# Building narrow one-hots as eight per-token instructions, and dropping a wait between dot products, in a PEER decoder layer

## The reference

```
q = (h @ w_query)                          # 8 heads, two halves of 128
s_top, i_top = top_k(q . sub_keys, 16)     # per head and half, of 128 keys
best, pos = top_k(s_top[0] + s_top[1], 16) # of the 16 x 16 pairs
expert = i_top[0] * 128 + i_top[1]         # 16384 experts
gate = softmax(best)
act = gelu(u[expert] . x)                  # u: 16384 x 2048
out = sum over 8 heads x 16 of gate * act * v[expert]   # v: 16384 x 2048
```

## Time and profile before

| what | value |
|---|---|
| median of 3 runs | 2019.93 us (2019.1 to 2022.46) |
| the profiled execution, its own time | 2017.72 us |
| its span in the trace | 2015.8 us |
| VectorE busy | 1363.1 us, 68% of the span |
| GpSimd busy | 1045.7 us, 52% |
| TensorE matmul busy | 1780.5 us, 88% |
| transfers | 647.28 MB |

### The profile page before, as it was taken

The page is one execution under the profiler, slowest core; times in us unless marked ns, Lnnn a source line. Parts: engine busy times, 40 slices in busy tenths (PEclk is TensorE's granted clock), DMA queues, the critical chain, the costliest instruction groups (busy, mean ns, idle before and its releaser), DMA issues.

```text
span 2015.8 us, 18828 instructions
## 1 busy us (share of the span) xinstructions
PE 1780.5 (88%) x6299; PEld 1127.8 (56%) x6299; DVE 1363.1 (68%) x2189; ACT 574.0 (28%) x1039; POOL 1045.7 (52%) x643
## 2 busy tenths in 40 slices
PE   7999999999999999875655588898887899999997
PEld 6888888888888898622222233444343554444442
DVE  5464453223334338898998888788888888887956
ACT  5445453345543520210000032233313730000001
POOL 4443343444432413575555555565556768876733
PEclk9999999999999999887777898999998999999999
DMA  8986455665545689999999999999999999999997
GB/s 211 242 176 145 146 188 149 196 195 181 169 154 184 196 278 407 376 412 420 414 420 417 402 404 396 409 403 412 400 413 416 393 381 406 405 410 380 402 422 313
DMA packets 157641, 647.28 MB, mean 321 GB/s; under 512 B 25894, under 2 KB 31086, under 8 KB 95598
## 3 DMA queue, kind: packets, MB, share of 16 engines
q0 software_dynamic: 73728, 450.98, 55.1%
q1 hardware_dynamic: 83824, 195.16, 31.1%
HBM read 729.91 MB, written 2.10 MB: 363 GB/s over the span
## 4 chain that ended last, share of the span: by engine, by line
PE 46%; DMA 25%; DVE 16%; issue 7%; POOL 6%; ACT 1%; SPq 0%; DVEq 0%; POOLq 0%; ACTq 0%
PE acc L1539 10%; PE acc L1541 10%; PE acc L1540 10%; DMA v_low<-in_peer_v_dram,idx 7%; DMA v_high<-in_peer_v_dram,idx 5%; DMA u_ring<-in_peer_u_dram,idx 5%; PE misc L1888 4%; PE acc L1868 3%; DVE y_sum L1420 3%; DMA v_more<-in_peer_v_dram,idx 2%; DVE u_ring L1386 2%; DVE u_ring L1388 2%; DMA u_mid<-in_peer_u_dram,idx 2%; PE acc L1829 1%; DMA late_hot<-in_peer_v_dram,idx 1%
## 5 line engine op out<-in xcount | busy, mean ns | idle before, releaser
L530 POOL TENSOR_TENSOR w_lo<-raw,w_hi 128x1024 fp32r<-128x1024 f32 x112 | 274.3, 2450 | 424.7 <-ACT w_hi L640 424.4
L1888 PE MATMUL misc<-v_high,diag 128*128 128x512 f32 x512 | 272.7, 683 | 99.7 <-DMA v_high<-in_peer_v_dram,idx 94.0
L1539 PE MATMUL acc<-w_hi,t_hi 128*128 128x512 f32 x896 | 354.9, 396 | 0.0
L1541 PE MATMUL acc<-w_hi,t_lo 128*128 128x512 f32 x896 | 349.3, 390 | 0.0
L1540 PE MATMUL acc<-w_lo,t_hi 128*128 128x512 f32 x896 | 348.7, 389 | 0.0
L1888 PE MATMUL misc<-v_low,diag 128*128 128x512 f32 x512 | 269.8, 679 | 85.8 <-DMA v_low<-in_peer_v_dram,idx 76.2
L988 DVE TENSOR_TENSOR w_lo<-raw,w_hi 128x1024 fp32r<-128x1024 f32 x112 | 154.2, 1377 | 265.0 <-ACT w_hi L640 264.9
L640 ACT ACTIVATE w_hi<-raw 128x1024 fp32r<-128x1024 f32 x224 | 236.9, 1059 | 329.9 <-PE acc L1541 283.8
L572 POOL DMA_INDIRECT u_ring<-in_peer_u_dram,idx x160 | 204.3, 1277 | 183.8 <-DVE dots L1388 121.3
L1888 PEld LDWEIGHTS misc<-v_high,diag 128*128 128x128 f32 x512 | 107.1, 219 | 250.9 <-DMA v_high<-in_peer_v_dram,idx 127.2
L1386 DVE CUSTOM_DVE_ANT_0 u_ring<-u_ring,hn 128x1024 f32<-128x1024 f32 x160 | 195.8, 1223 | 68.4 <-DMA u_ring<-in_peer_u_dram,idx 60.4
(11 more groups left out here) (273 smaller groups left out, 2170.3 us busy)
## 6 DMA issues: line engine op xcount, KB each, us to landing
u_ring<-in_peer_v_dram SPq DMA_DIRECT2D x48, 1024.0 KB, 8.9
raw<-in_w_in_dram SPq DMA_DIRECT2D x64, 512.0 KB, 6.7
raw<-in_xattn_wk_dram SPq DMA_DIRECT2D x32, 512.0 KB, 4.4
raw<-in_xattn_wv_dram SPq DMA_DIRECT2D x32, 512.0 KB, 3.9
raw<-in_w_out_dram SPq DMA_DIRECT2D x32, 512.0 KB, 4.7
raw<-in_xattn_wq_dram SPq DMA_DIRECT2D x32, 512.0 KB, 4.7
raw<-in_xattn_wo_dram SPq DMA_DIRECT2D x32, 512.0 KB, 4.8
praw<-in_peer_wq_dram SPq DMA_DIRECT2D x24, 512.0 KB, 7.2
```

The lines of the kernel that those rows point to most:

```text
L530: nc.gpsimd.tensor_tensor(w_lo[:, j % RING, :, :], raw[:, j % RING, :, :], w_hi[:, j % RING, :, :].bitcast(F32), ALU.subtract).then_inc(lo ...
L1539: nc.tensor.matmul(o, xh, w_hi[:, s, kk, :], start=first, stop=False)
L1541: ins = nc.tensor.matmul(o, xl, w_hi[:, s, kk, :], start=False, stop=last)
L1888: ins = nc.tensor.matmul(o, diag[:, n % 4, :], v_slot(n % VS)[:, i * CW:(i + 1) * CW], start=False, stop=False)
```

## The change

In a batch, VectorE made `hotB` with two instructions over [rows, 8, 48]: compare the token's first key (broadcast over 48) with the keys (broadcast over 8 tokens), wait for that, and multiply by the weight (broadcast over 48), in place. Now there are eight instructions, one for each token, over [rows, 48]: each reads one tensor operand, the keys, compares it with a scalar per partition, the token's first key, and multiplies by a second scalar per partition, its weight. There is no wait between them, and the last raises `hot_ready`. The wait for `dot_done` in the last three groups is gone.

```diff
-                step(nc.vector.tensor_tensor(hotB[0:rows, q, :, :], listsT[0:rows, 0, t:t + WB].unsqueeze(2).to_broadcast([rows, WB, DENSE]),
-                                             keys[0:rows, FROM:].unsqueeze(1).to_broadcast([rows, WB, DENSE]), ALU.is_equal))
-                nc.vector.tensor_tensor(hotB[0:rows, q, :, :], hotB[0:rows, q, :, :],
-                                        listsT[0:rows, 2, t:t + WB].unsqueeze(2).to_broadcast([rows, WB, DENSE]),
-                                        ALU.mult).then_inc(hot_ready, 1)
+                for i in range(t, t + WB):
+                    ins = nc.vector.tensor_scalar(hotB[0:rows, q, i - t, :], keys[0:rows, FROM:], listsT[0:rows, 0, i:i + 1], listsT[0:rows, 2, i:i + 1],
+                                                  ALU.is_equal, ALU.mult)
+                ins.then_inc(hot_ready, 1)
...
                     dve.wait_ge(u_landed[u_index(n)], 16 * u_turn(n))
-                    if g >= GROUPS - WHOLE - 1:
-
-                        dve.wait_ge(dot_done, n)
```

## The result

The changed kernel takes 2032.4 us as the median of 6 runs (2030.56 to 2034.19), the kernel before 2019.9 us (2017.12 to 2022.46): a ratio of 1.006, 95% interval 1.005 to 1.0071, 12.5 us slower by the medians. The forecast was 2020.4 us, no change, with a range to 2027. The profiled execution took 2034.19 us, its span is 2032.3 us.

What follows compares the result with a forecast made beforehand. Transfers on the 16 DMA engines were taken as the bound. At 1607 us, 4.0 - 0.35 - 4.1 = -0.4 us, nothing late; +0.5 taken from 0 to +2.4 gave 2020.4 us after 2019.93, range 2015.5 to 2027.

Steps and rivals of the forecast that it cites:

- What bounds the kernel: From near 800 us the expert part waits for transfers; groups 14 and 15 lose only 2.2 us of full transfer.
- The prediction's own sign of being wrong: A DMA share under 0.95 in groups 14 and 15 would show the forecast wrong; 0.97 and more, right.
- The removed wait: Between neighbouring dots of groups 13 to 15: 0.05 us each, 1.0 us in all, 0.35 before 1607 us; can't lose.
- the sum: VectorE's lateness at 1607 us: 4.0 - 0.35 - 4.1 = -0.4 us, +1.8 at the top; overall 0 to +2.4.
- The cost of a batch: Eight narrow instructions at 0.18 us take 1.44 us against 1.06 before: +0.4 us a batch.
- Where it falls: Block 0's sixteen batches, 6.4 us more, cost nothing under waits for `u`; block 1's first ten add 4.0 us.
- the 4.1 us of slack: VectorE's waits in block 1 before 1607 us: 2.3 for GELU, 0.5 for TensorE, about 1.3 for `u`.
- Rival B: Slower: VectorE and GpSimd hold each other up at batches in groups 14 and 15; +4.6 us, 2025 us; chance 0.09.
- A: Slower: the eight instructions do not overlap, 0.3 us each, +1.3 us a batch; +10 us, 2030 us; chance 0.07.
- C: Faster: the scalars cost nothing, a batch takes 0.65 us, -0.41; about 2017.7 us; chance 0.17.
- D: Only the order of gathers shifts, moving others a few us either way; beyond 2 us to either side, chance 0.09.

Runs made afterwards that it cites:

- e1: Kernel before with only the wait for dot_done removed, old pair of one-hot instructions kept; 2025.73 us, ratio 1.003.
- e12: Changed kernel with one wait added after each eight narrow instructions of block 1; 2024.12 us, ratio 1.0024.
- e7: Changed kernel with one scalar per partition instead of two, weight left out, so it does not compute the layer; 2026.81 us, ratio 1.0035.
- e2: Kernel before with only the eight narrow instructions put in, wait for dot_done kept; 2023.4 us, ratio 1.0016.
- e6: Kernel before, all waits kept, with three extra narrow instructions into an unused place ahead of each pair; 2022.62 us, ratio 1.0014.
- e5: Kernel before with the eight narrow instructions, wait for dot_done kept, and one more wait after the fourth of the eight; 2027.3 us, ratio 1.0034.
- e9: Kernel before without the wait between dots, with one wait after each pair of block 1 instead; 2019.99 us, ratio 1.0.
- e8: Kernel before without the wait between dots, dot halves in groups 14 and 15 plain one-tensor sums, not computing the layer; 2018.67 us, ratio 0.9992.

## Why the prediction was wrong

- **What bounds the kernel: right.** Transfers do, and most of the loss went where VectorE has no cover, into groups 14 and 15: 12.1 us more of lost transfer time. The prediction's own sign of being wrong, a DMA share under 0.95 there, came with 0.86 and 0.88.
- **The removed wait: the step that failed.** "So it is worth 0.05 us", and "It can't lose". Both are wrong. The size came from a gap of 0.18 us in group 12, taken for the state without the wait. The changed kernel still shows 0.20 us at that place, so something else made it, most likely the wait for the row of `u`; between neighbouring dots of group 14 its gap is 0.00, so the wait had been worth 0.23 us at each pair of dots. And it can lose, because GpSimd needed that gap: the term stood in the sum as 0.35 us won, and the runs show about 6 us lost (e1; 7.6 us between the changed kernel and e12). The argument for "can't" looked at VectorE's own slots alone, and not at the engine that issues the gathers.
- **The cost of a batch: right in kind, at the top of its range.** Forecast 0.18 us an instruction, between 0.145 and 0.21; measured 0.21. The second scalar costs nearly what the first does (e7). A batch is 1.71 - 1.06 = 0.65 us longer, not 0.4. (The lower value should read 0.14: 0.08 us for 128 columns makes 0.05 for 80. It changes nothing here.)
- **Where it falls: block 0's batches are free**, as forecast. The DMA share from 1190 to 1530 us is 1.00 in both kernels; VectorE is busy 9.3 us longer there (282.02 against 272.74) and waits 6.9 us less for `u` (47.9 against 54.8 over all its slots). Group 14 starts with its lists copied at 1536.93 against 1534.84 us, the 2.1 us that the first group had already. In block 1 the 4.1 us of slack hid less than counted: in e2 the last dot is summed at 1642.8 us, 3.3 us later than before, and the added work costs about 3 us (e2, e6), where the sum had 0 to 2.4.
- **Rival B named the right pair of engines and the wrong instructions.** It had VectorE's narrow instructions wait for GpSimd, or the reverse, for up to 1.4 us a batch. In fact GpSimd waits for the dots behind a batch, and these were there all along. A sign of it stood in the trace before, issues of 0.95 us beside others of up to 3.35 us; the prediction did not ask what made them long. It gave B 0.09 and 2025 us.
- **Rivals A and C: ruled out.** The eight do overlap (0.21 us from start to start, a median of 304 ns each), and the scalars are not free. A's time, 2030 us, is near the measured one, but not by A's cause: e2 and e6, which have the added work alone, lose some 3 us. D, a chance shift of the order, does not account for issues that grow and shrink with the gaps.

What stays open is why e5 is slower than e2, whether the second read, the row written back or something else in the dot is what blocks, and why it blocks beyond one instruction only behind a batch. The two halves measured alone leave some 3 us of the 12.5 unassigned, within their intervals.

## What to carry to other kernels

A wait on a busy VectorE is not only a cost: where GpSimd issues the gathers, a gap ahead of a row of long two-operand instructions can decide whether an issue gets out within the row or only at its end. One wait at each of the places where such a row begins can do as much as a wait before every instruction (e9). Before a wait is removed, compare GpSimd's issue durations with the shortest of their kind, and lay the long ones beside VectorE's timeline. To measure what a wait is worth, take the gap without it from a place where no other wait stands in the same spot. Many narrow instructions with scalars per partition replace one wide one only if their fixed parts, here 0.21 us for 48 columns, sum to less.

## What the hardware showed that was not expected

- A GpSimd gather issue that takes 0.95 us alone took up to 6.00 us while VectorE ran two-operand instructions of 1024 columns with no gap behind a batch, and ended 0.90 to 0.96 us after the last of them.
- A short gap was enough: 0.15 us from the end of the accumulator read to the next dot in the kernel before, and in e9 only 0.03 us behind a pair (1560.14 + 0.55 to 1560.72); with one of these at each of 16 batches in 110 us no issue took over 2.03 us. Behind such a gap four dot halves in a row let an issue in between two of them (e9, 1566.84).
- Back-to-back sums of one tensor, equally long, did not delay issues at all (e8, 1.24 us at most).
- The second scalar per partition adds about 0.056 us to a VectorE instruction (e7), the first 0.064 us.
